# Top-k turns of tiles 4 to 7: out of the memory stage, into the loops of the early attention

## What is computed

```python
idx = relu(einsum('bthd,bsd->bths', qi, ki))            # indexer
score = einsum('bths,bth->bts', idx, wi)
score = where(k_pos // CHUNK <= pos // CHUNK, score, -inf)
sel_score, sel = top_k(score, topk)                     # topk = 256 for the prompt
logits = einsum('btgrd,btkgd->btgrk', qg, k[sel]) * HEAD_DIM ** -0.5
p = softmax(where(isfinite(sel_score), logits, -inf))
```

## Time and profile before

| | us |
|---|---|
| median of 3 runs | 3965.82 |
| lowest and highest | 3963.68, 3971.33 |
| the profiled execution | 3972.68 |
| its span | 3970.9 |
| stage 2, group B early (from the trace) | 277 to 486 |
| stage 3, group A early | 486 to 653 |
| stage 4, `sparse_mixer` | 653 to 1084 |

### The profile page before, as it was taken

How to read it: one execution, slowest core, us unless ns; L and a number is a source line. 1 busy time by engine, 2 the same in 40 slices (tenths; PEclk the granted TensorE clock), 3 DMA queues, 4 the chain that set the end, 5 groups by cost and what they waited for, 6 DMA issues and landing times. The chain is left out here.

```text
span 3970.9 us, 49760 instructions
## 1 busy us (share of the span) xinstructions
PE 3476.7 (88%) x17237; PEld 2503.3 (63%) x17237; DVE 2466.1 (62%) x5779; ACT 1067.4 (27%) x2008; POOL 1958.6 (49%) x1478
## 2 busy tenths in 40 slices
PE   7889887998899888987878878888589999999998
PEld 4445555788878667766656666765456656656655
DVE  3764423656857677779889797898634433444434
ACT  1213333121156523222222222233222212222222
POOL 0000001224400144778888888765266777777773
PEclk9888987998999999999999999999899999999999
DMA  3002103312431235799999999979898998999996
GB/s 117 10 33 61 55 29 122 101 54 88 144 91 33 92 119 186 283 357 389 399 395 397 401 394 400 363 247 405 318 352 317 387 364 338 383 347 348 350 366 224
DMA packets 335401, 978.46 MB, mean 246 GB/s; under 512 B 34400, under 2 KB 84456, under 8 KB 333648
## 3 DMA queue, kind: packets, MB, share of 16 engines
q0 software_dynamic: 156672, 570.49, 36.8%
q1 hardware_dynamic: 173584, 389.78, 27.9%
q10 hardware_dynamic: 4928, 15.34, 1.1%
HBM read 873.61 MB, written 101.89 MB: 246 GB/s over the span
## 5 line engine op out<-in xcount | busy, mean ns | idle before, releaser
L1606 PE MATMUL n_ps<-n_xh_flat,n_wh 128*128 128x512 f32 x3072 | 750.5, 402 | 159.9 <-POOL n_wh L1596 158.0
L2862 PE MATMUL e_y_ps<-e_wh,e_vh 128*128 128x512 f32 x3072 | 750.2, 400 | 45.1 <-DVE e_wh L2986 33.9
L1606 PEld LDWEIGHTS n_ps<-n_xh_flat,n_wh 128*128 128x128 f32 x3072 | 582.1, 192 | 323.9 <-POOL n_wh L1596 200.7
L2862 PEld LDWEIGHTS e_y_ps<-e_wh,e_vh 128*128 128x128 f32 x3072 | 571.7, 189 | 265.7 <-issue 133.4
L1025 POOL CAST m_wh<-raw 128x1024 fp32r<-128x1024 f32 x40 | 42.2, 1054 | 909.7 <-issue 657.7
L2946 POOL TENSOR_TENSOR e_vh<-raw,e_vh 128x1024 fp32r<-128x1024 f32 x128 | 309.8, 2423 | 228.4 <-ACT e_vh L2888 224.4
L3025 DVE TENSOR_TENSOR oT<-e_y_ps,oT 128x512 f32<-128x512 f32 x256 | 176.0, 691 | 379.9 <-PE e_y_ps L2862 253.3
L2543 POOL DMA_INDIRECT e_rows<-in_v,eid x346 | 348.6, 1008 | 97.5 <-issue 87.3
L1596 POOL TENSOR_TENSOR n_wh<-raw,n_wh 128x1024 fp32r<-128x1024 f32 x128 | 306.9, 2398 | 40.4 <-ACT n_wh L1591 38.5
L1943 DVE CUSTOM_DVE_ANT_0 oT<-oT,n_row_ps 128x1024 f32<-128x1024 f32 x227 | 271.1, 1217 | 66.4 <-DMA oT<-in_u,eid 60.6
L1062 PE MATMUL m_ps<-m_xh_flat,m_wh 128*128 128x272 f32 x1920 | 262.6, 299 | 40.2 <-DVE oT L1095 11.7
(11 more groups left out here) (387 smaller groups left out, 5610.8 us busy)
## 6 DMA issues: line engine op xcount, KB each, us to landing
raw<-in_ut SPq DMA_DIRECT2D x128, 512.0 KB
raw<-in_v SPq DMA_DIRECT2D x126, 512.0 KB
s_hid<-flat SPq DMA_DIRECT2D x128, 256.0 KB
xrow<-s_hid SPq DMA_DIRECT2D x126, 256.0 KB
s_gate<-g_stage SPq DMA_DIRECT2D x3, 8192.0 KB, 53.4
raw<-in_w_pq SPq DMA_DIRECT2D x32, 512.0 KB
m_ring<-s_gate SPq DMA_DIRECT2D x32, 512.0 KB
gh<-s_gate SPq DMA_DIRECT2D x32, 512.0 KB
```

Source lines behind the costliest of these rows:

```text
L1606: mm = pe.matmul(self.ps[:, n % 2, 0:ND], self.uh[:, at % 2, a, k * P:(k + 1) * P], self.xd[:, b, k, :], start=(k == 0 and o == 0), stop=( ...
L2862: mm = pe.matmul(y_ps[:, o, 0:TD], vh[:, n % SLOT, a, m * P:(m + 1) * P], wh[n % SLOT][:, b, g * TD:(g + 1) * TD], start=(c == 0 and e == ...
```

## The change

The 24 late rounds leave `sparse_mixer`. They are done in the loops of stages 2 and 3, three rounds of the four tiles (twelve turns) in each of the four iterations of both (`LATE_ROUNDS = (3, 3)`). `late_by` says how many turns are done by which unit: in stage 2 four ahead of `row_max(0)` and one behind each of the units 0 to 7, in stage 3 two ahead of `row_max(0)` and one behind each of the ten units. The masks of the late tiles are made at the end of stage 3. Each loop has two semaphores of its own for it, which belong to those that GpSimd clears; the two of `sparse_mixer` go.

```diff
+LATE_ROUNDS = (3, 3)
...
+        late_best = sb("late_best", [P, len(LATE), 8])
...
+        late_picked, late_dropped = S("late_picked"), S("late_dropped")
+        late_turns = [t for r in range(LATE_ROUNDS[0 if fox else 1]) for t in LATE]
+        late_beside = [0] * NU
+        for i in range(len(late_turns) - (4 if fox else 2)):
+            late_beside[i % NU] += 1
+        late_by = [len(late_turns) - sum(late_beside[u:]) for u in range(NU + 1)]
...
+            dve.sem_inc(late_dropped, len(LATE))
...
+                def select_late(n_turn):
+
+                    t = late_turns[n_turn]
+                    s, top = score_of(keep, t), late_best[:, t - LATE[0], :]
+                    dve.wait_ge(late_dropped, j * len(late_turns) + n_turn + 1)
+                    dve.sem_inc(passed, 1)
+                    dve.max(top, s).then_inc(late_picked, 1)
+                    dve.wait_ge(late_picked, j * len(late_turns) + n_turn + 1)
+                    dve.sem_inc(passed, 1)
+                    dve.match_replace(s, top, s, TAKEN).then_inc(late_dropped, 1)
+
                 if fox:
 
                     for n_turn in range(done_by[0]):
                         select(n_turn)
+                for n_turn in range(late_by[0]):
+                    select_late(n_turn)
...
                     if fox:
                         for n_turn in range(done_by[u], done_by[u + 1]):
                             select(n_turn)
-
+                    for n_turn in range(late_by[u], late_by[u + 1]):
+                        select_late(n_turn)
+
+            if not fox:
+                dve.wait_ge(late_dropped, 4 * len(late_turns) + len(LATE))
+                for t in LATE:
+                    s = score_of(keep, t)
+                    dve.tensor_scalar(s, s, -2e38, NEG, ALU.is_gt, ALU.mult)
...
             for n in range(MIX, 4):
-                select(2)
                 mx.add_out(dve, n)
...
             for n in range(4, QRY):
                 mx.add_out(dve, n)
-                select(1)
             norm_q.means(dve)
-            select(12)
             for k in range(KD):
-                select(1)
                 mx.split_gained(dve, k)
             norm_q.finish(dve)
             dve.wait_ge(norm_q.normed, norm_q.all)
             for n in range(QRY, ATT):
-                select(1)
                 mx.scale_q(dve, n)
             mx.attend_dve(dve)
             for n in range(ATT, PKQ):
-                select(1)
                 mx.add_out(dve, n)
             norm_f.dve(dve)
             dve.wait_ge(norm_f.normed, norm_f.all)
             mx.make_x(dve)
-            select(len(turns))
-            dve.wait_ge(dropped, len(turns))
-            for t in LATE:
-                s = score_of(keep, t)
-                dve.tensor_scalar(s, s, -2e38, NEG, ALU.is_gt, ALU.mult)
```

More of the change, by code:

```diff
@@ L209 @@
 ROUNDS_A = 8
+LATE_ROUNDS = (3, 3)
+assert 4 * sum(LATE_ROUNDS) == ROUNDS - ROUNDS_A
 def mix_inputs(nc, sem, dram, keep):
@@ L1300, in sparse_mixer @@
         norm_f = mx.norm()
-        best = sb("best", [P, len(LATE), 8])
-        picked, dropped = sems["picked"], sems["dropped"]
         block = ctx.enter_context(nc.Block())
@@ L1478, in _ @@
         def _(dve):
-            turns = [t for r in range(ROUNDS - ROUNDS_A) for t in LATE]
-            n_turn = [0]
-            def select(count):
-                for n in range(n_turn[0], min(n_turn[0] + count, len(turns))):
-                    s, top = score_of(keep, turns[n]), best[:, turns[n] - LATE[0], :]
-                    if n >= len(LATE):
-                        dve.wait_ge(dropped, n - len(LATE) + 1)
-                    dve.max(top, s).then_inc(picked, 1)
-                    dve.wait_ge(picked, n + 1)
-                    dve.match_replace(s, top, s, TAKEN).then_inc(dropped, 1)
-                n_turn[0] = min(n_turn[0] + count, len(turns))
             dve.memset(ones[:, :], 1.0).then_inc(set_, 1)
```

2 lines of the change are left out of this document (1 added, 1 removed).

## The result

| | before | changed |
|---|---|---|
| median, us | 3967.85 (4 runs) | 4086.34 (4 runs) |
| lowest and highest | 3963.68, 3971.33 | 4081.60, 4089.65 |
| span of the profiled execution | 3970.9 | 4084.5 |
| mean granted clock of TensorE | 0.952 | 0.931 |

The ratio is 1.0291, with a 95% interval of 1.0272 to 1.0310: slower by 118.5 us on the medians and by 113.6 us between the two profiled executions. The median lies inside the range of the prediction. Its sum, 127.5, is 9 us above the difference of the medians and 14 above that of the profiles.

The account below looks back on a forecast made before the run. It took VectorE as the bound in stage 2's units, and in stage 3's once turns are added. 69.7 + 55.8 + 2.7 + 0.3 - 5.3 + 4.3 = +127.5 us on 3965.8 gave 4093.3 us, range 4078 to 4110.

Parts of the forecast that it names:

- a round at 8.23: Low end of a turn's price: four tiles' turns at stage 4's 8.23 us instead of 8.71; stage 3 given as 51.6.
- stage 2, two rounds behind the units: Eight turns an iteration between stage 2's units count in full, four ahead of `row_max(0)` are free: +69.7 us.
- stage 3, iterations: Two turns ahead of the first `row_max` and one behind each unit lengthen an iteration by 13.96 us: +55.8 us.
- end of stage 3: One turn and the masks behind the last reciprocal, +2.7 us; four more semaphores for GpSimd to clear, +0.3 us.
- stage 4, two waits: TensorE no longer waits for turns ahead of `add_out` (-3.59) and the first `scale_q` (-1.66): -5.3 us.
- clock in the projections, seven groups: First 48 projection matmuls after each series of units run more at low clock, 17.1 us a group: +4.3 us.
- The rival of the idle time: Turns fill VectorE's idle time in stages 2 and 3, so only stage 4 changes: 3960.5 us, faster; chance 0.01.
- The rival of TensorE: TensorE at half clock bounds stage 3's units, up to 3 us more an iteration: up to 4105 us; chance 0.14.

Follow-up runs that it names:

- e1: Changed kernel with all twelve late turns of a stage 2 iteration ahead of `row_max(0)`, stage 3 as changed: 4021.26 us, 1.0127 of before.
- e8: Changed kernel with stage 2's twelve late turns all ahead of `row_max(0)`, none in stage 3, twelve rounds ending stage 4: 3976.41 us, 0.9974 of before.
- e7: Changed kernel with every turn, tiles 2 and 3's own included, moved out of the units, twelve rounds ending stage 4: 3975.83 us, 0.9959 of before.
- e10: e7 plus useless matmuls where TensorE waits in the loops of stages 2 and 3: 3948.23 us, 0.9943 of before.
- e12: The kernel before with the same useless matmuls as e10 added alone: 3958.67 us, 0.9969 of before.
- e6: Changed kernel with eight late turns at the start of each stage 3 iteration and one behind units 0 to 3: 4081.41 us, 1.0247 of before.

## Why the prediction was right, and where its terms were off

The mechanism was the predicted one, and the forecast of 4093.3 is 7 us above the median of 4086.3. The 3965.8 that it started from was the median of the earlier runs; from 3967.85 the same sum gives 4095.4, 9 us too much. Nearly all of its errors have one sign, and the low end of its range is 112 us over its start: the 113.6 us between the profiles would just have been inside. Two of its small sums are off: seven groups at 17.1 us are +4.2 and not +4.3, and with a round at 8.23 stage 3 is 50.6 and not 51.6. Its terms against the profiled executions:

| term | predicted | measured | from |
|---|---|---|---|
| stage 2, two rounds behind the units | +69.7 | +68.1 | TensorE's units, four series |
| stage 3, iterations | +55.8 | +51.5 | the same |
| end of stage 3 | +2.7, +0.3 | +3.6 | TensorE's wait, 9.89 to 13.44 |
| stage 4, two waits | -5.3 | -9.1 | stage 4's length |
| clock in the projections, seven groups | +4.3 | -0.8 | their sum, 115.5 to 114.7 |
| not in the sum | 0 | +0.3 | up to stage 2 +3.1, behind stage 4 -3.3, first group of stage 2 +0.5 |
| sum | +127.5 | +113.6 | |

**Stage 2.** That VectorE bounds the units, and that the eight turns count in full, held: the four series from the first scores to the next projections are 16.38, 17.19, 17.30 and 17.27 us longer, where 17.42 was predicted. The first grew less because it had been 1 us longer than the others before. That the four turns ahead of `row_max(0)` are free held as well, and e1 showed that twelve are. The rival of the idle time didn't come about. The Trainium skill (Perfetto Trace Analysis, section "Optimization Strategy") says that interleaving regimes with different most-contended engines may improve a kernel; this one interleaves two such regimes and is slower by 2.9%. The same section's next advice is to find the gaps on the engine that one optimizes for, and what ends them. Read so for VectorE, it leads to e1 and e8, and the traces agree: in the gap ahead of `row_max(0)` 48 turns cost nothing.

**Stage 3.** The steps on VectorE were right (23.23 us against 23.39 for the ten reciprocals; the first `row_max` came 3.68 us later against 3.45). The mis-sized term is the tail that I added unchanged to them: from the tenth reciprocal to the next projection it was 2.31 us before and is 1.30 now. Before, the last unit's product came behind the tenth reciprocal, in the third iteration:

```profile
610.33 0.41 PE L724 MATMUL d_o_ps<-vnat,d_pt 128*32 128x64 f32 x4 [0.46 <-ACT oT L758]
```

In the changed kernel, that product is done by the time VectorE gets to the reciprocal, and only a scaling, a transpose and the copy are left:

```profile
717.99 0.64 PE L733 MATMUL d_o_ps<-vnat,d_pt 128*32 128x64 f32 x4 [0.46 <-ACT oT L767]
...
719.59 0.30 ACT L815 ACTIVATE d_opair<-d_o_ps,d_rinv 32x64 f32<-32x64 f32 x1 [1.46 <-DVE d_rinv L948]
720.03 0.28 PE L699 MATMUL d_o_ps<-con,d_opair 32*128 32x32 f32 x1 [1.41 <-ACT d_opair L815]
...
720.65 0.95 PE L667 MATMUL d_s_ps<-xn,wq 128*128 128x352 f32 x1 [0.34 <-issue]
```

That is 1.0 us an iteration, 4 in all, and it is the term of the stage that was mis-sized. The prediction took VectorE's chain as the bound and then kept a tail from a time when TensorE's chain ended later.

**End of stage 3.** The turn and the masks stand behind the last reciprocal as predicted. The masks end at 778.77, 3.54 us behind ScalarE's last copy at 775.23, where the prediction had 2.7; the difference is the same tail, since the copy now comes 1.0 us sooner after the reciprocal. GpSimd's first cast starts 5.70 us behind the masks, against 5.4 before: the 0.3 us of four more semaphores came as predicted, and in every profile the figure is 5.4 without them and 5.7 with them.

```profile
775.03 0.20 ACT L767 ACTIVATE oT<-d_o_ps 128x32 f32 x1 [0.56 <-PE d_o_ps L699]
...
776.67 2.10 DVE L959 TENSOR_SCALAR m_ring<-m_ring 128x640 f32<-128x640 f32 x4
...
784.47 1.35 POOL L1055 CAST m_wh<-raw 128x1024 fp32r<-128x1024 f32 x1 [784.01 <-issue]
```

**Stage 4.** The two waits of TensorE fell by 3.4 and 1.7 us, close to the 3.6 and 1.7 predicted. The other 4 us are groups with the same number of matmuls that took less time. In the changed kernel:

```profile
807.29 4.66 PE L1092 MATMUL m_ps<-m_xh_flat,m_wh 128*128 128x272 f32 x24 [6.61 <-DVE oT L1125]
...
882.94 7.17 PE L1405 MATMUL m_ps<-m_q_flat,m_keys 128*128 128x256 f32 x32 [2.33 <-DMA m_keys<-in_w_mk]
...
930.74 39.52 PE L1092 MATMUL m_ps<-m_xh_flat,m_wh 128*128 128x272 f32 x312 [2.04 <-DVE m_q_flat L1132]
```

Before they took 5.81, 8.86 and 41.03 us, for the 32 matmuls in the middle by this row:

```profile
760.94 8.86 PE L1377 MATMUL m_ps<-m_q_flat,m_keys 128*128 128x256 f32 x32 [2.06 <-DMA m_keys<-in_w_mk]
```

Together -4.35, and +0.43 for the first 48. The granted clock goes with them: over these three groups it was 0.50, 0.81 and 0.96 before, and 0.67, 1.00 and 1.00 in the changed kernel. The sum held the waits and left out the clock behind them. But the length of the wait doesn't decide it. In e7 the first group takes 5.81 us behind a wait of 6.60 and the middle one 8.86 behind 2.34, where the changed kernel has 4.66 behind 6.61 and 7.17 behind 2.33. The third takes 39.5 us behind 2.04 in nine kernels, and 41.03 behind the same 2.04 in e8 and e10. What decides it isn't shown, and I know no way to foresee it. In the kernels here stage 4 comes out between 421.4 and 426.6 with the three turns gone.

**The clock term** was wrong in its sign and its reason. I expected the projections to be slower after longer units. The clock in the units did fall, in the third series of stage 2 from 1.00 to 0.54, and in that of stage 3 from 0.87 to 0.72. A window of one series of stage 2's units before:

```profile
414.00:433.00 19.00, 16.36 (x97) 10.89 (x97) 16.07 (x59) 12.29 (x46) 0.00 (x0) 1.00 0.56 158
```

and one series each of stages 2 and 3 in the changed kernel:

```profile
449.00:486.00 37.00, 26.85 (x97) 18.54 (x97) 32.50 (x84) 12.62 (x49) 0.00 (x0) 0.54 0.28 81
685.00:721.00 36.00, 20.98 (x98) 14.70 (x99) 32.17 (x75) 12.62 (x47) 0.00 (x0) 0.72 0.09 30
```

But that costs nothing there, since VectorE is the bound, and the projections didn't start slower than before. In the second iteration of stage 2 they begin at 329.16 and at 349.15, and the clock came back after 6 us and after 4. Windows of TensorE before (stretch, busy us, PEclk, DMA):

```profile
333.00:335.00 2.00, 2.00 (x5) 0.50 0.00 0
335.00:337.00 2.00, 2.00 (x8) 0.95 0.00 0
```

and in the changed kernel:

```profile
351.00:353.00 2.00, 2.00 (x5) 0.50 0.00 0
353.00:355.00 2.00, 2.00 (x9) 1.00 0.00 0
```

The prediction said of the Trainium skill (TensorE: Matmul & The Clock Gate, section "What's actually happening") that by its rule the term is at its slow end. That the clock falls in the thinner units is as the rule has it; my step from there to the projections was not, for they began at the low clock before too. The same section puts the price of the ramp under 1% of a typical kernel. No run here measures that price; e12 got back 0.31% with its filling.

**The rival of TensorE** as the bound of stage 3's units didn't come about in the changed kernel, where VectorE idles only 1.29 us from the rotation on. It was real all the same: in e6 (stage 3) and e7 (stage 2) series at a lower clock took 3.5 and 3.3 us more as soon as VectorE had room.

**What stays open.** What brings the clock down isn't settled: e10 and e12 show that filling the waits as a set holds it, not which of the three places is needed, and in two of e7's four series the clock stayed up behind the same waits. Each filler was tried in one size only. In the totals, e10 and e12 gain by more than their stages 2 and 3 alone: of e10's 22 us, 11 lie in stages 2 and 3 and 9 in stage 4, where the three turns are gone too and where the rest varies by itself.

## What to carry to other kernels

Idle time is a place, not a sum: before moving work to an engine that is "41% busy", look in its own order at what stands behind the point where it would go, and put it only where the next instruction waits for something else. Twelve turns ahead of the first row maximum cost nothing, and eight of them behind the units cost 17 us an iteration. When a chain on one engine grows until it is the bound, take the tail behind it anew, because what ended it before may have been another engine's. And where TensorE is the bound and its granted clock is under 1.00, look at the waits ahead of the fall: in this kernel useless matmuls in them gave 0.3%.

## What the runs showed of the hardware

- Behind waits of TensorE of 1.31 and 0.41 us the granted clock fell from 1.00 to 0.50 for some 6 us in two of e7's four series, which took 20.5 us, and not in the other two, of 17.24 and 18.40. With the 1.31 us filled (e10) it was 0.95 to 0.99 in all four, and the two long ones took 17.1.
- The clock behind a wait isn't a function of its length: behind 2.04 us, 312 matmuls took 39.52 us in the changed kernel and 41.03 in e10. Within one kernel it may repeat: the two profiles of before agree on stage 4 within 0.5 us.
- The 1.2 GHz of TensorE cost nothing where VectorE was the bound: 36 us more busy time in stage 2 are in none of its lengths.
- Between two dependent VectorE instructions, a wait on a register's value with a semaphore increment behind it left 0.15 us, and a wait on a constant alone 0.03, a turn being 0.11 us longer; at half the width the gap was the same.
- Four more semaphores to clear on GpSimd moved its first cast from 5.4 to 5.7 us behind the end of the stage before.
